# Row numbers of a paged gather moved one stage forward, and the sample rows' gate product moved ahead of a transpose

## The chip, the cores and the metric

The kernel is one program on one core of a Trainium2 chip. The metric is device time in microseconds (us), the median of the runs. Lower is better.

## The reference, cut to what matters

One layer of a hybrid decoder works on 2048 prompt rows and on 32 sample rows (8 entries of 4 new tokens, each with a past of 8192 tokens held in 64 pages of 128 tokens).

```python
k_past = cache_k_sb[i][page_table].reshape(dec_b, past, N_HEADS_SB, HEAD_DIM)
v_past = cache_v_sb[i][page_table].reshape(dec_b, past, N_HEADS_SB, HEAD_DIM)
...
o_sb = _stick_breaking(qa, k_all, v_all, pos_s, kpos_s, sb_bias[i])
...
def _merge(x, o_sb, z_sb, o_dl, z_dl, p, ...):
    y_sb = _rmsnorm(o_sb, out_norm_sb) * silu(z_sb)      # 512 columns
    y_dl = _rmsnorm(o_dl, out_norm_dil) * silu(z_dl)     # 512 columns
    x = x + einsum('bse,ed->bsd', concatenate([y_sb, y_dl]), w_out)
    gate = sigmoid(einsum('bsd,de->bse', x, w_ple_gate))
    return x + gate * einsum('bsp,pd->bsd', p, w_ple)
```

The paged keys and values of the sample rows are found through `page_table`. Every row, prompt or sample, then goes through the merge.

## The kernel before

The program runs seven stages one after the other: two projections, stick-breaking attention of the prompt (`sbp`), dilated attention of the prompt (`dil`), stick-breaking attention of the sample rows over the paged cache (`sbs`), dilated attention of the sample rows (`dls`), and the merge. A stage is a block in which each engine has its own ordered list of instructions, tied to the others by semaphores. All engines meet at a barrier between two stages, so nothing of a stage runs before the last engine has left the one ahead. Only the buffer `held` and a few semaphores live across stages.

**Dilated prompt stage (`dil`).** It goes over 80 work items g: four head pairs of 20 items each. In step g of its list, TensorE turns the weights of item g (L1363), scores item g + 2 (L1381, L1390), weighs item g - 1 (L1409) and turns out the sum of item g - 2 (L1418). VectorE in the same step copies turned weights (L1223), takes the maxima of item g + 2 (L1233), scales and writes out item g - 2 (`put_out`, L1267) and copies the sum of item g - 1 (`take_out`, L1254, L1258). TensorE waits for that last copy (`oT_copied`) before it opens the next sum in the bank `O`. GpSimd reorders the turned queries and keys for the next head pair (L1183, four casts of 128x2048) and issues the output transfers of each branch. SyncE (SP) issues the loads. At its start SP issues ident, masks, the values of two branches and the odd queries and keys, and then waits.

**Paged sample stage (`sbs`).** GpSimd gathers pages with indirect transfers of 128 rows of 8 KB each (L1560), into rings of eight slots for keys and eight for values. The row numbers come from the tile `rows`: SP loads the page table spread over 128 partitions (L1545) and a lane number for each partition (L1547); VectorE casts the table to floating point in four pieces of 32 partitions (L1582) and makes `page * 32 + lane` (L1585); GpSimd waits for that before its first gather. VectorE only then goes on with its own list: two memsets (L1587, L1588), the padded queries (L1600), and a short chain with ScalarE and TensorE over the new tokens (L1604 to L1624). TensorE multiplies padded queries and new keys (L1776) and, when that chain is through, starts to turn the gathered keys (L1793). Then come 32 steps of turning, scoring (L1837), a cumulative sum, exponentials and weighing (L1825).

**Merge.** Tile 0 holds the 32 sample rows, tiles 1 to 16 hold 128 prompt rows each. `prepare(i)` on VectorE and ScalarE makes y(i) out of loaded inputs (from L2332 to L2367). TensorE turns y(i) (L2556, `turn_y`), multiplies with w_out in two halves (`project_out`, `merge_Out`), turns x1(i) and p(i) (`turn_x1`, `turn_p`), and multiplies with w_ple_gate and w_ple (`gate_ple`, 48 matmuls into `merge_Gate` and 12 into `merge_Ple`). Every product is split in three (L2548 to L2550). All three kinds of transposes share one pair of banks, `merge_T`, which ScalarE (L2481) and VectorE (L2375, `low`) copy out. The order on TensorE in step i is:

```python
turn_x1(i - 1); project_out(i, 0); turn_p(i - 1); project_out(i, 1)
turn_y(i + 1)
gate_ple(i - 1)
```

`turn_x1(i)` waits for the residual sums of tile i (L2390). `turn_p(i)` waits for `low` of x1(i), which frees the first bank. VectorE's order in step i is `final_min(i - 2)` (L2396), `final_max(i - 2)` (L2401), `low` of x1(i - 1), `final_sum(i - 2)`, `low_p(i - 1)`, `low` of y(i + 1), `residual(i)`, `prepare(i + 2)`. In step 1 `prepare(2)` stands before `low` of y(2). ScalarE's list has the matching order, with the exponential of the gate product (`gate_in`) behind `prepare`.

Of the kernel before, what the change touches and what calls it, by code (L numbers as in the profile page):

```python
# [6 lines left out]
F32 = mybir.dt.float32  # L7
# [968 lines left out]


def paged_constants(held):
# [25 lines left out]

def dilated_prompt(nc, t, held, dil_qk_loaded, paged_loaded):

# [59 lines left out]
    with ctx:  # L1066
# [16 lines left out]
        lse = m.sb("lse", [P, 2, TILES, 2])  # L1083
        o_out = m.sb("o_out", [P, 2, TILES, P])
        Z = m.ps("Z", [P, 4, 512])
        ps_T = m.ps("ps_T", [P, 2, 512])
# [4 lines left out]
        masks_loaded = m.sem("masks_loaded")  # L1091
        consts_r = m.sem("consts_r")
        v_loaded = m.sems("v_loaded", 2)
        qk_odd_loaded = m.sem("qk_odd_loaded")
# [30 lines left out]
        def _(sp):  # L1125
# [11 lines left out]
            load_v(1)  # L1137
            load_dilated_qk(sp, t, qk_odd, 1, qk_odd_loaded)
            sp.wait_ge(turned, FILLS)
            load_dilated_qk(sp, t, held, 2, dil_qk_loaded)  # L1140
# [66 lines left out]
        def _(dve):  # L1207
# [52 lines left out]
            def put_out(g):  # L1260
# [4 lines left out]
                if x4 == 0 and b >= 2:  # L1265
# [4 lines left out]
                                        .to_broadcast([P, 8, DH]), ALU.mult).then_inc(o_scaled, 1)  # L1270

            for f in range(FILLS):
                low(0, f, Z[:, f % 4, :])
            for g in range(-2, G + 2):
                if 0 <= g < G and not short(g):
                    copy_weights(g)
# [174 lines left out]

def stick_breaking_sample(nc, t, held, paged_loaded):

# [15 lines left out]
    with ctx:  # L1469
# [3 lines left out]
            views[n] for n in ("ident", "own", "pick", "newer", "every", "spread", "bias", "fresh", "qk_new", "v_new"))  # L1473
        every_table = m.sb("every_table", [P, DEC_B * PAGES], I32)
        page_f = m.sb("page_f", [P, DEC_B * GROUPS])
        rows = m.sb("rows", [P, DEC_B * GROUPS], I32)
        lane = m.sb("lane", [P, 1])
        ones = m.sb("ones", [P, CK])
# [25 lines left out]

        lanes_loaded = m.sem("lanes_loaded")
        rows_step = m.sem("rows_step")
        zeroed = m.sem("zeroed")
# [35 lines left out]
        @block.sync  # L1543
        def _(sp):
            sp.dma_start(every_table[:, :], t["page_table"].rearrange("b n -> (b n)").rearrange("(a n) -> a n", a=1)  # L1545
                         .to_broadcast([P, DEC_B * PAGES])).then_inc(lanes_loaded, 16)
            sp.dma_start(lane[:, :], t["lane"][:, :]).then_inc(lanes_loaded, 16)  # L1547
            for b in range(DEC_B):
                sp.wait_ge(row_copied, b + 1)
                sp.dma_start(t["o_sb_s"][b * DEC_S:(b + 1) * DEC_S, :], o_row[:, :]).then_inc(stored, 16)  # L1550
            sp.wait_ge(stored, 16 * DEC_B)

        @block.gpsimd
        def _(pool):
            pool.wait_ge(rows_step, 2)

# [21 lines left out]
        def _(dve):  # L1578
            dve.wait_ge(lanes_loaded, 32)
            for i in range(GP):  # L1580
                r = slice(LANES * i, LANES * (i + 1))
                pages = nc.vector.tensor_copy(page_f[r, :], every_table[r, :].rearrange("p (n g) -> p g n", g=GP)[:, i, :])  # L1582
            pages.then_inc(rows_step, 1)
            dve.wait_ge(rows_step, 1)
            nc.vector.tensor_scalar(rows[:, :], page_f[:, :], float(LANES), lane[:, 0:1], ALU.mult, ALU.add) \  # L1585
                .then_inc(rows_step, 1)
            nc.vector.memset(q_pad[:, :, :], 0.0).then_inc(zeroed, 1)  # L1587
# [550 lines left out]
def merge(nc, t):  # L2138
# [6 lines left out]
    with ctx:  # L2145
# [396 lines left out]
        def _(pe):  # L2542
# [74 lines left out]
            for i in range(N + 1):  # L2617
# [6 lines left out]
                if i < N:  # L2624
                    project_out(i, 1)
                if i + 1 < N:
                    turn_y(i + 1)
                if i >= 1:
                    gate_ple(i - 1)


def build(nc, t):
# [8 lines left out]
    with nc.semaphore("tick") as tick:  # L2641
# [4 lines left out]
        paged_loaded = nc.alloc_semaphore(name="paged_loaded")  # L2646
        with nc.sbuf_tensor("held", [P, 2 * TILES * P], F32) as held:
# [3 lines left out]
            dilated_prompt(nc, t, held, dil_qk_loaded, paged_loaded)  # L2651
            stick_breaking_sample(nc, t, held, paged_loaded)
        nc.clear_and_free_semaphores([dil_qk_loaded, paged_loaded] + ahead_loaded + pair_loaded)
        nc.all_engine_barrier()
# [78 lines left out]
```

## Time and profile before

| what | value |
|---|---|
| median of 3 runs | 3076.78 us (3069.73 to 3077.31) |
| the profiled execution's own time | 3099.58 us |
| its span | 3097.9 us |
| TensorE busy in the span | 2808.1 us (91%) |
| VectorE, ScalarE, GpSimd busy | 1572.5, 1344.4, 749.7 us |
| mean granted TensorE clock | 0.959 of full speed |

The span is the part of the profiled execution between its first and its last instruction; 1.7 us lie around it. The profiled execution is 22.8 us longer than the median of the runs that were not profiled. Busy shares are means over seven stages with different limits.

### The profile page before, as it was taken

To read this page: it belongs to the slowest core of one execution; us is meant where nothing else is said; L and a number is where in the kernel's file an instruction comes from. 1 tells how busy PE (TensorE), PEld (TensorE's weight loads), DVE (VectorE), ACT (ScalarE), POOL (GpSimd) and SP (SyncE) were. 2 spreads that over 40 slices of the span, in tenths; PEclk is the share of its full clock that TensorE was granted. 3 is DMA by queue.
4 is the path that set the end of the run, shared out by engine and by line. 5 is a ranking of instruction groups with operands and counts; after the bars stand their busy time and mean duration, and the time that the engine had idled before them with its cause. 6 is when DMAs were issued, how large, how long until landed. Compare 5 with 4: busy or idle time off the path is not lost. (4 is left out here: it accounts for less than half of the span.)

```text
span 3097.9 us, 47359 instructions
## 1 busy us (share of the span) xinstructions
PE 2808.1 (91%) x17542; PEld 1978.9 (64%) x17542; DVE 1572.5 (51%) x2730; ACT 1344.4 (43%) x2482; POOL 749.7 (24%) x952
## 2 busy tenths in 40 slices
PE   7999989999899999998999758888888774899998
PEld 5888858888655555554888645555555442688887
DVE  3000032222588888887777633444434335666663
ACT  3212131111487777786677523333333323333332
POOL 0000001111122222223577733333333100000000
PEclk9999999999899999999999969999999987899999
DMA  6565766556300000103333389999999695323321
GB/s 209 200 215 197 235 209 210 183 203 217 112 15 28 15 28 1 42 8 100 97 84 84 80 339 407 416 419 417 408 414 407 252 374 217 126 100 108 108 87 43
DMA packets 209768, 574.16 MB, mean 185 GB/s; under 512 B 40096, under 2 KB 109184, under 8 KB 173728
## 3 DMA queue, kind: packets, MB, share of 16 engines
q0 software_dynamic: 45568, 348.22, 28.9%
q1 hardware_dynamic: 164000, 223.27, 21.9%
q8 instruction: 126, 2.06, 0.3%
q14 instruction: 74, 0.61, 0.1%
HBM read 494.67 MB, written 143.73 MB: 206 GB/s over the span
## 5 line engine op out<-in xcount | busy, mean ns | idle before, releaser
L495 PE MATMUL proj_ps_G<-proj_w_hi,proj_xT_hi 128*128 128x512 f32 x1024 | 399.8, 390 | 1.6 <-DVE proj_xT_lo L352 1.6
L499 PE MATMUL proj_ps_G<-proj_w_hi,proj_xT_lo 128*128 128x512 f32 x1024 | 398.6, 389 | 0.0
L497 PE MATMUL proj_ps_G<-proj_w_lo,proj_xT_hi 128*128 128x512 f32 x1024 | 398.5, 389 | 0.0
L1632 DVE COPY sbs_kT<-sbs_ps_T 128x512 f32<-128x512 f32 x256 | 173.7, 687 | 360.1 <-PE sbs_ps_T L1793 351.1
L434 ACT ACTIVATE proj_out<-proj_ps_G,proj_stat 128x512 f32<-128x512 f32 (+1 forms) x136 | 93.4, 688 | 579.5 <-PE proj_ps_G L499 574.8
L1793 PE MATMUL sbs_ps_T<-held,sbs_k_ring 128*128 128x128 f32 x2048 | 284.0, 297 | 26.8 <-ACT sbs_kT L1714 17.8
L1793 PEld LDWEIGHTS sbs_ps_T<-held,sbs_k_ring 128*128 128x128 f32 x2048 | 254.0, 155 | 64.2 <-issue 33.5
L695 POOL CAST sbp_sp_hi<-sbp_sp 128x512 fp32r<-128x512 f32 (+3 forms) x320 | 171.9, 551 | 455.8 <-DVE sbp_sp L742 455.6
L742 DVE SCALAR_TENSOR_TENSOR sbp_sp<-sbp_Z,sbp_el 128x512 f32<-128x512 f32 (+3 forms) x320 | 180.7, 606 | 88.9 <-ACT sbp_el L824 88.5
L495 PEld LDWEIGHTS proj_ps_G<-proj_w_hi,proj_xT_hi 128*128 128x128 f32 x1024 | 192.3, 188 | 41.4 <-DVE proj_xT_lo L352 1.8
L499 PEld LDWEIGHTS proj_ps_G<-proj_w_hi,proj_xT_lo 128*128 128x128 f32 x1024 | 192.2, 188 | 39.9
L497 PEld LDWEIGHTS proj_ps_G<-proj_w_lo,proj_xT_hi 128*128 128x128 f32 x1024 | 192.3, 188 | 39.3
L1714 ACT ACTIVATE sbs_kT<-sbs_ps_T 128x512 f32<-128x512 f32 x256 | 145.3, 591 | 152.8 <-PE sbs_ps_T L1793 151.7
L819 ACT ACTIVATE sbp_el<-sbp_Z 128x1024 f32<-128x1024 f32 (+3 forms) x160 | 143.6, 898 | 122.4 <-PE sbp_Z L908 121.2
L748 DVE TENSOR_TENSOR sbp_sp_lo<-sbp_sp,sbp_sp_hi 128x512 fp32r<-128x512 f32 (+3 forms) x320 | 192.0, 639 | 0.0
L352 DVE TENSOR_TENSOR proj_xT_lo<-proj_ps_T,proj_xT_hi 128x512 fp32r<-128x512 f32 (+1 forms) x34 | 21.1, 663 | 318.0 <-ACT proj_xT_hi L421 318.0
L1560 POOL DMA_INDIRECT sbs_v_ring<-in_cache_v_sb,sbs_rows x128 | 120.1, 939 | 256.5 <-PE sbs_O L1825 226.5
L1560 POOL DMA_INDIRECT sbs_k_ring<-in_cache_k_sb,sbs_rows x128 | 121.3, 948 | 168.9 <-PE sbs_ps_T L1793 139.2
L824 ACT ACTIVATE sbp_el<-sbp_el 128x1024 f32<-128x1024 f32 (+3 forms) x160 | 148.0, 925 | 0.0
L946 PE MATMUL sbp_L<-sbp_a,sbp_v_all 128*64 128x512 f32 (+3 forms) x640 | 145.8, 533 | 2.4 <-DVE sbp_LE L761 0.9
L831 ACT ACTIVATE sbp_a<-sbp_Z 128x1024 f32<-128x1024 f32 (+3 forms) x160 | 143.4, 896 | 9.9 <-PE sbp_Z L923 3.5
L1321 ACT ACTIVATE dil_sc<-dil_Z,dil_keep 128x256 f32<-128x256 f32 (+1 forms) x320 | 140.3, 462 | 3.2 <-DVE dil_keep L1233 3.2
(305 smaller groups left out, 5694.0 us busy)
## 6 DMA issues: line engine op xcount, KB each, us to landing
out_k_win_s<-in_cache_k_win POOLq DMA_DIRECT2D x16, 2044.0 KB
out_v_win_s<-in_cache_v_win POOLq DMA_DIRECT2D x16, 2044.0 KB
dls_k_in<-in_cache_k_win SPq DMA_DIRECT2D x16, 1024.0 KB, 10.7
dls_v_in<-in_cache_v_win SPq DMA_DIRECT2D x16, 1024.0 KB, 14.6
proj_out<-in_w_in SPq DMA_DIRECT2D x28, 512.0 KB, 5.0
merge_o<-scratch_o_dil SPq DMA_DIRECT2D x48, 256.0 KB, 4.8
proj_x_in<-in_x_prompt SPq DMA_DIRECT2D x16, 512.0 KB, 4.4
scratch_xT_hi<-proj_xT_hi SPq DMA_DIRECT2D x16, 512.0 KB, 4.8
```

The lines of the kernel that those rows point to most:

```text
L495: nc.tensor.matmul(ps_G[0:n, g, :], xT_hi[:, slot, k, 0:n], w_hi[:, k, cols], start=(k == 0), stop=False)
L497: nc.tensor.matmul(ps_G[0:n, g, :], xT_hi[:, slot, k, 0:n], w_lo[:, k, cols], start=False, stop=False)
L499: mm = nc.tensor.matmul(ps_G[0:n, g, :], xT_lo[:, slot, k, 0:n], w_hi[:, k, cols], start=False, stop=(k == KC - 1))
L695: nc.gpsimd.tensor_copy(sp_hi[:, b, h, c:512], sp_[:, g % 3, h, c:512]).then_inc(hi_done, 1)
L742: nc.vector.scalar_tensor_tensor(out=sp_[:, g % 3, h, c:512], in0=Z[:, z(g), h, c:512], scalar=LINEAR, in1=el[:, b, h, c:512], op0=ALU.max ...
L748: nc.vector.tensor_tensor(sp_lo[:, b, h, c:512], sp_[:, g % 3, h, c:512], sp_hi[:, b, h, c:512].bitcast(F32), ALU.subtract).then_inc(lo_do ...
L824: nc.scalar.activation(el[:, g % 2, :, c:512], el[:, g % 2, :, c:512], ACT.Ln, bias=1.0).then_inc(ln_done, 1)
L946: mm = nc.tensor.matmul(L[h * DH:(h + 1) * DH, c:512], v_all[:, j, p * P + h * DH:p * P + (h + 1) * DH], a[:, g % 2, h, c:512], start=True ...
L1560: pool.indirect_dma_start(ring[:, q % RING, :, :].rearrange("p g c -> p (g c)"), None, pages[0].rearrange("n (s g) h d -> (n s) (g h d)", ...
L1632: nc.vector.tensor_copy(kT[:, j, i, :], ps_T[:, x % TB, :]).then_inc(kT_odd, 1)
L1714: nc.scalar.activation(kT[:, j, i, :], ps_T[:, x % TB, :], ACT.Copy).then_inc(kT_even, 1)
L1793: tr = nc.tensor.transpose(by_lane[:, g_in, :], k_ring[:, q % RING, g_in, i * P:(i + 1) * P], ident[:, :])
```

## The change

Two edits. The first moves the making of the row numbers: `rows` becomes a buffer that lives across stages, the two loads are issued by SP in the dilated stage behind its first loads, and VectorE makes the numbers there at the top of step g = 20. The paged stage starts without them. The second edit puts `gate_ple(0)` ahead of `turn_y(2)` in step 1 of the merge. All other steps keep their order.

```diff
 def dilated_prompt(nc, t, held, rows, dil_qk_loaded, paged_loaded, rows_ready):
...
             load_dilated_qk(sp, t, qk_odd, 1, qk_odd_loaded)
+            sp.dma_start(every_table[:, :], t["page_table"].rearrange("b n -> (b n)").rearrange("(a n) -> a n", a=1)
+                         .to_broadcast([P, DEC_B * PAGES])).then_inc(lanes_loaded, 16)
+            sp.dma_start(lane[:, :], t["lane"][:, :]).then_inc(lanes_loaded, 16)
             sp.wait_ge(turned, FILLS)
...
+            def page_rows():
+                dve.wait_ge(lanes_loaded, 32)
+                for i in range(PAGES_A_GATHER):
+                    r = slice(PAGE // PAGES_A_GATHER * i, PAGE // PAGES_A_GATHER * (i + 1))
+                    pages = nc.vector.tensor_copy(page_f[r, :], every_table[r, :].rearrange("p (n g) -> p g n", g=PAGES_A_GATHER)[:, i, :])
+                pages.then_inc(pages_done, 1)
+                dve.wait_ge(pages_done, 1)
+                nc.vector.tensor_scalar(rows[:, :], page_f[:, :], float(PAGE // PAGES_A_GATHER), lane[:, 0:1], ALU.mult, ALU.add) \
+                    .then_inc(rows_ready, 1)
...
             for g in range(-2, G + 2):
+                if g == 20:
+                    page_rows()
                 if 0 <= g < G and not short(g):
                     copy_weights(g)
...
 def stick_breaking_sample(nc, t, held, rows, paged_loaded, rows_ready):
...
         def _(sp):
-            sp.dma_start(every_table[:, :], t["page_table"].rearrange("b n -> (b n)").rearrange("(a n) -> a n", a=1)
-                         .to_broadcast([P, DEC_B * PAGES])).then_inc(lanes_loaded, 16)
-            sp.dma_start(lane[:, :], t["lane"][:, :]).then_inc(lanes_loaded, 16)
...
         def _(pool):
-            pool.wait_ge(rows_step, 2)
+            pool.wait_ge(rows_ready, 1)
...
         def _(dve):
-            dve.wait_ge(lanes_loaded, 32)
-            for i in range(GP):
-                r = slice(LANES * i, LANES * (i + 1))
-                pages = nc.vector.tensor_copy(page_f[r, :], every_table[r, :].rearrange("p (n g) -> p g n", g=GP)[:, i, :])
-            pages.then_inc(rows_step, 1)
-            dve.wait_ge(rows_step, 1)
-            nc.vector.tensor_scalar(rows[:, :], page_f[:, :], float(LANES), lane[:, 0:1], ALU.mult, ALU.add) \
-                .then_inc(rows_step, 1)
             nc.vector.memset(q_pad[:, :, :], 0.0).then_inc(zeroed, 1)
...
                 if i < N:
                     project_out(i, 1)
+                if i == 1:
+                    gate_ple(0)
                 if i + 1 < N:
                     turn_y(i + 1)
-                if i >= 1:
+                if i > 1:
                     gate_ple(i - 1)
```

## Rows read from the trace of the kernel before

**Rows 1.** The page, part 1: busy time, share of the span and instructions.

```profile
PE 2808.1 (91%) x17542; PEld 1978.9 (64%) x17542; DVE 1572.5 (51%) x2730; ACT 1344.4 (43%) x2482; POOL 749.7 (24%) x952
```

**Rows 2.** Waits of the paged stage, 1900 to 2400 us: total, times, longest.

```profile
POOL sbs_k_ring L1560 <- PE sbs_ps_T L1793: 98.8, 59, 4.1
...
PE sbs_ps_T L1793 <- ACT sbs_kT L1714: 12.5, 24, 0.5
```

**Rows 3.** Windows of the paged stage: busy time, instructions, clock, DMA share, GB/s.

```profile
1808.00:1813.00 5.00, 0.00 (x0) 0.00 (x0) 1.93 (x7) 0.83 (x2) 0.00 (x0) 0.50 1.02 428
...
2000.00:2100.00 100.00, 84.47 (x684) 52.12 (x682) 42.42 (x70) 33.86 (x62) 37.15 (x40) 0.98 1.01 419
```

**Rows 4.** Timeline where the paged stage begins: start, duration, engine, line; idle time and releaser.

```profile
1787.93 1.28 ACT L62 ACT_TABLE_LOAD   x1 [24.89 <-PEq L45]
...
1791.35 1.09 DVE L1582 CAST sbs_page_f<-sbs_every_table 32x128 f32<-32x128 int32 x4 [21.47 <-DMA sbs_lane<-in_lane]
1792.48 0.29 DVE L1585 TENSOR_SCALAR sbs_rows<-sbs_page_f,sbs_lane 128x128 int32<-128x128 f32 x1
1792.98 1.12 DVE L1587 MEMSET sbs_q_pad<- 128x1280 f32 x1 [0.21 <-issue]
1793.05 1.06 POOL L1560 DMA_INDIRECT sbs_k_ring<-in_cache_k_sb,sbs_rows  x1 [10.84 <-DVE sbs_rows L1585]
```

**Rows 5.** Timeline, the end of the paged stage's opening chain.

```profile
1809.97 0.47 DVE L1604 TENSOR_SCALAR sbs_zn<-sbs_ps_T,held 32x256 f32<-32x256 f32 x1 [11.57 <-DMA proj_rope<-in_rope]
...
1817.01 1.33 PE L1793 MATMUL sbs_ps_T<-held,sbs_k_ring 128*128 128x128 f32 x5 [0.64 <-DVE sbs_aT_new L1624]
```

**Rows 6.** Timeline where the next stage (`dls`) begins.

```profile
2477.95 1.28 ACT L62 ACT_TABLE_LOAD   x1 [2.99 <-PEq L2654]
2478.28 1.12 DVE L1991 MEMSET dls_q_pad<- 128x1280 f32 x1 [5.02 <-PEq L2654]
```

**Rows 7.** Dilated stage: one window, then the timeline around step g = 20.

```profile
1529.00:1604.00 75.00, 75.00 (x832) 62.53 (x831) 58.58 (x103) 51.84 (x188) 55.03 (x51) 1.00 0.37 100
...
1532.85 7.82 POOL L1183 CAST dil_D_hi<-dil_T_hi 128x2048 fp32r<-128x2048 f32 x2
1534.62 0.64 DVE L1223 COPY dil_pT<-dil_ps_T 128x512 f32<-128x512 f32 x1
...
1537.77 0.68 DVE L1254 COPY dil_oT<-dil_O 128x512 f32<-128x512 f32 x1
...
1539.31 0.88 PE L1409 MATMUL dil_O<-dil_pT,dil_v_br 128*64 128x128 f32 x12
...
1540.61 7.86 POOL L1183 CAST dil_D_lo<-dil_T_lo 128x2048 fp32r<-128x2048 f32 x2
```

**Rows 8.** Timeline, a VectorE instruction of 256 elements in the paged stage.

```profile
1814.15 0.28 DVE L1619 TENSOR_SCALAR sbs_an<-sbs_an 32x256 f32<-32x256 f32 x1
```

**Rows 9.** Timeline of TensorE in the merge, steps 1 and 2.

```profile
2647.97 0.39 PE L2550 MATMUL merge_Out<-merge_wo_hi,merge_yT_lo 128*128 128x512 f32 x1
2659.16 1.97 PE L2556 MATMUL merge_T<-merge_ident,merge_y 128*128 128x128 f32 x8 [10.80 <-DVE merge_y L2367]
...
2675.55 1.03 PE L2556 MATMUL merge_T<-merge_ident,merge_x 128*128 128x128 f32 x8
...
2681.89 0.38 PE L2556 MATMUL merge_T<-merge_ident,merge_p_in 128*128 128x128 f32 x2
...
2687.59 1.03 PE L2556 MATMUL merge_T<-merge_ident,merge_y 128*128 128x128 f32 x8
2688.38 0.47 PE L2548 MATMUL merge_Gate<-merge_wg_hi,merge_xT_hi 128*128 128x512 f32 x1
...
2702.11 1.03 PE L2556 MATMUL merge_T<-merge_ident,merge_x 128*128 128x128 f32 x8
```

**Rows 10.** Timeline of VectorE in the merge, step 2.

```profile
2691.26 0.16 DVE L2332 TENSOR_TENSOR merge_top<-merge_lse 128x8 f32<-128x8 f32 x1
...
2704.30 1.28 DVE L2375 TENSOR_TENSOR merge_xT_lo<-merge_T,merge_xT_hi 128x512 fp32r<-128x512 f32 x2
```

More of the change, by code:

```diff
@@ L975, in load_dilated_qk @@
         sp.dma_start(view[:, i, :, :], src.rearrange("(n p) c -> p n c", p=P)[:, :, p * P:(p + 1) * P]).then_inc(loaded, 16)
+PAGES_A_GATHER = 4
+GROUPS_OF_PAGES = PAGES // PAGES_A_GATHER
 def paged_constants(held):
@@ L1002, in load_paged_constants, with dilated_prompt @@
             .then_inc(loaded, 16)
-def dilated_prompt(nc, t, held, dil_qk_loaded, paged_loaded):
+def dilated_prompt(nc, t, held, rows, dil_qk_loaded, paged_loaded, rows_ready):
     DILS = (1, 4, 16)
@@ L1084, in dilated_prompt @@
         o_out = m.sb("o_out", [P, 2, TILES, P])
+        every_table = m.sb("every_table", [P, DEC_B * PAGES], I32)
+        page_f = m.sb("page_f", [P, DEC_B * GROUPS_OF_PAGES])
+        lane = m.sb("lane", [P, 1])
         Z = m.ps("Z", [P, 4, 512])
@@ L1092, in dilated_prompt @@
         consts_r = m.sem("consts_r")
+        lanes_loaded = m.sem("lanes_loaded")
+        pages_done = m.sem("pages_done")
         v_loaded = m.sems("v_loaded", 2)
@@ L1449, in _, with stick_breaking_sample @@
                         turn_in(p + 1, f, OB[:, :])
-def stick_breaking_sample(nc, t, held, paged_loaded):
+def stick_breaking_sample(nc, t, held, rows, paged_loaded, rows_ready):
     C = H * DEC_S
@@ L1473, in stick_breaking_sample @@
             views[n] for n in ("ident", "own", "pick", "newer", "every", "spread", "bias", "fresh", "qk_new", "v_new"))
[L1474 to L1477, printed above, removed]
         ones = m.sb("ones", [P, CK])
@@ L1503, in stick_breaking_sample @@
         R = m.ps("R", [P, 512])
-        lanes_loaded = m.sem("lanes_loaded")
-        rows_step = m.sem("rows_step")
         zeroed = m.sem("zeroed")
@@ L2646, in build @@
         paged_loaded = nc.alloc_semaphore(name="paged_loaded")
-        with nc.sbuf_tensor("held", [P, 2 * TILES * P], F32) as held:
+        rows_ready = nc.alloc_semaphore(name="rows_ready")
+        with nc.sbuf_tensor("held", [P, 2 * TILES * P], F32) as held, \
+                nc.sbuf_tensor("rows", [P, DEC_B * GROUPS_OF_PAGES], I32) as rows:
             project(nc, t, 0, held, ahead_loaded, pair_loaded)
@@ L2650, in build @@
             stick_breaking_prompt(nc, t, held, pair_loaded, dil_qk_loaded)
-            dilated_prompt(nc, t, held, dil_qk_loaded, paged_loaded)
-            stick_breaking_sample(nc, t, held, paged_loaded)
-        nc.clear_and_free_semaphores([dil_qk_loaded, paged_loaded] + ahead_loaded + pair_loaded)
+            dilated_prompt(nc, t, held, rows, dil_qk_loaded, paged_loaded, rows_ready)
+            stick_breaking_sample(nc, t, held, rows, paged_loaded, rows_ready)
+        nc.clear_and_free_semaphores([dil_qk_loaded, paged_loaded, rows_ready] + ahead_loaded + pair_loaded)
         nc.all_engine_barrier()
```

## The prediction

> **What bounds the kernel now.** I read the page first. TensorE is busy for 91% of the span and VectorE for 51% [rows 1], but that is a mean over seven stages, and both edits touch places where TensorE stands still. So I went on by stage.
>
> In the paged stage the DMA engines are full (share 1.01, 419 GB/s) and TensorE is busy for 84 of 100 us [rows 3]. The waits tell which of the two paces it: GpSimd's gathers wait for TensorE's turned keys (98.8 us in 500), while TensorE's own waits are ended by ScalarE, VectorE or nothing that shows, none of them by a gather [rows 2]. The full DMA share follows the steps, it does not set them. Either way the stage has a fixed length from its opening on, so time saved in the opening comes off the end.
>
> The opening: the barrier lets the engines go at 1787.93, where ScalarE loads its table. VectorE has nothing to do until the lane numbers land at 1791.35, makes the row numbers until 1792.77, and only at 1792.98 begins the memset that heads its own chain. GpSimd's first gather goes at 1793.05 [rows 4]. The chain ends with the first turned key at 1817.01, which waited for VectorE (`sbs_aT_new`) and not for the gather issued 24 us earlier [rows 4, 5].
>
> In the dilated stage TensorE is busy for 75.00 of 75 us around step g = 20 and VectorE for 58.58 [rows 7]. TensorE is the bound; VectorE has some 16 us of slack in 75.
>
> In the merge TensorE stands still for 10.80 us ahead of `turn_y(2)`, waiting for y(2) [rows 9].
>
> **Edit 1, the row numbers.** *What goes from the paged stage*: two loads and five VectorE instructions. The next stage shows what an opening without them looks like: ScalarE's table load at 2477.95 and the same memset of 128x1280 at 2478.28, 0.33 us later [rows 6]. So the memset moves from 1792.98 to 1787.93 + 0.33 = 1788.26: 4.72 us earlier. The first gather moves by about as much, so the gathers, the memsets and the padded queries keep their places relative to each other. What would be late next is the first key: it has the same 24 us as before. Bounds: at most 1792.98 - 1787.93 = 5.05 us, at least nothing, if something else holds the chain. I take 4.7.
>
> The chain holds one stretch I cannot explain: VectorE waits 11.57 us until 1809.97 for the small product of L1776, while the DMA engines are full at 428 GB/s [rows 3, 5]. I leave it as long as it is; a rival takes it up.
>
> *What comes to the dilated stage*: SP issues two more loads behind its first ones, ahead of a wait that it reaches in either case; the numbers are wanted only in the second quarter of the stage's 80 items. VectorE gets the same five instructions: 1792.77 - 1791.35 = 1.42 us [rows 4]. They stand ahead of the copy at 1534.62, so that `take_out(19)`, seen at 1537.77, is pushed back. VectorE loses part of the 1.42 us again in its own short waits (0.29 and 0.32 us between these two), so about 0.65 us is left: the copy ends at 1537.77 + 0.68 + 0.65 = 1539.10. TensorE wants it at 1539.31 [rows 7]. Cost 0 by 0.2 us; if no wait were given back it would be 1.42 - (1539.31 - 1538.45) = 0.56 us. Cover gone altogether: 1.42 us. I take 0. GpSimd waits on a semaphore that has long been set.
>
> One cover could be false. From 1532.85 to 1548.47 GpSimd runs its four casts of some 3.9 us [rows 7], next to the moved VectorE instructions; in the old place it stood idle. The Trainium skill ("SBUF — State Buffer", section "SBUF: two separate sides") says that VectorE and GpSimd share a port pair under an exclusive lock, which a VectorE copy, cast or tensor_scalar takes in its two-port mode, and that the loser blocks for the whole instruction. By that rule the sum would lose up to what rival A gives, if these five ran in that mode. The rows speak against it: the five take 0.26 to 0.29 us for 128 elements a lane [rows 4], and a tensor_scalar with twice as many takes 0.28 [rows 8], so the moved ones run at half the rate of that one, one element at a time. A duration from the old place should hold.
>
> **Edit 2, the gate product ahead of `turn_y(2)`.** *What fills the idle time*: TensorE is through with `project_out(1, 1)` at 2648.2 [rows 9]. `gate_ple(0)` has what it needs by then (x1, p and all weights are split) and takes 2702.11 - 2688.38 = 13.73 us at full clock: 48 + 12 matmuls at 0.229 us [rows 9]. It ends at 2661.9. y(2) was ready at about 2659.1, so `turn_y(2)` starts at 2661.9, 2.8 us later than before.
>
> *What is late next.* In the old order `gate_ple(0)` lay over the work that ScalarE and VectorE do behind `turn_y(2)`. Now nothing does. VectorE's list is strict: low of y(2), residual(1), prepare(3), final_min(0), final_max(0), low of x1(1). In a warm step prepare begins 2691.26 - 2687.59 = 3.67 us after the turn starts, and low of x1 begins 2704.30 - 2691.26 = 13.04 us after that [rows 9, 10]. From 2661.9:
> - `turn_x1(1)` waits for residual(1): 2661.9 + 3.7 = 2665.6, so TensorE idles 2.9 us behind the turn. It then turns and does half a projection, 2681.89 - 2675.55 = 6.3 us [rows 9], until 2671.9.
> - `turn_p(1)` waits for low of x1(1), first half: 2661.93 + 3.67 + 13.04 + 0.69 = 2679.3. TensorE idles 7.4 us more.
>
> Before, `turn_p(1)` stood at 2681.89. So the idle 10.80 us come back as 2.9 + 7.4 = 10.3 us, and the gain up to here is 2681.9 - 2679.4 = 2.5 us, most of it the slow start of the old order: from 2659.16 the same work took 2675.55 - 2659.16 = 16.39 us against 2702.11 - 2687.59 = 14.52 us [rows 9], 1.87 us lost at half clock (1.2 instead of 2.4 GHz) after the idle stretch. A new idle stretch of 7 us should cost the same again. Net 2.5 - 1.9 = 0.6 us. Bounds: a gain of 2.5 us if the clock holds, a loss of 2 x 1.87 - 2.5 = 1.2 us if the slow stretch costs twice what it cost before. From `turn_y(3)` on the order and the slack are those of before.
>
> **Sum.** 4.7 - 0.0 + 0.6 = 5.3 us. The profiled execution, 3099.58 us, would be 3094.3. It lies 22.8 us above the median of the unprofiled runs; I take the difference over as it is: 3076.8 - 5.3 = 3071.5 us. A measurement of this kernel tells about 0.3%, or 9.2 us, from no change.
>
> **The rivals.**
>
> *A, the port (ends slower).* The five VectorE instructions are held until GpSimd's four casts are through: from 1534.6 to 1548.5, 13.9 us, less the 1539.31 - 1538.45 = 0.9 us that TensorE has. TensorE loses 13.0 us in a stage that it bounds; with the gain of 5.3 the time is 3076.8 + 13.0 - 5.3 = 3084.5. It decides the sign from a hold of 6.2 us on; a hold by one cast (3.9 us) leaves a gain of 2. For it: the casts do lie there. Against it: the durations above. By the Trainium skill's rule on the exclusive port pair the same 3084.5 follows if the mode is the two-port one.
>
> *B, the opening does not move.* Something else, such as the start of the first gathers beside the memset, holds the chain, and 1817.01 stays. Then only the merge's 0.6 us is left: 3076.2. Against it: the next stage opens without delay [rows 6].
>
> *C, the unexplained wait goes too.* If the wait until 1809.97 was a matter of how the chain meets the full DMA engines, it may shrink with another placing. Worth up to some 8 of its 11.57 us: 3076.8 - 5.3 - 8 = 3063.5. Against it: gathers and chain move together.
>
> *D, the merge's idle stretch is gained in full.* If VectorE and ScalarE kept up, TensorE would be late by the 2.9 us only: 10.8 + 1.9 - 2.9 = 9.8 us instead of 0.6, and 3062.3 in all. Against it: VectorE's 13.04 us, which no edit shortens.
>
> **How the numbers follow.** My forecast 0.70 (its own range 3067 to 3075.5, for a median of a few runs that spread over 7.6 us), A 0.05, B 0.11, C 0.08, D 0.04, other things 0.02. The range from 3063.5 to 3078.5 takes in the forecast and B and the near part of C, and leaves out D, A and the far part of C: under 2 in 10. Faster by over 0.3%: C and D, 0.12, and 0.03 for a forecast that measures long, 0.15. Slower by over 0.3%: A gives 0.25%, so only its upper part and chance, 0.04. Within: 0.81.
>
> **What would show it.** In the profile after: no VectorE instruction of L1582 or L1585's kind in the paged stage, its memset 0.3 us behind the table load and the first gather next to it; the distance from memset to first turned key 24.0 us as before. In the dilated stage the five instructions at 0.26 to 0.29 us, and TensorE without a gap behind them (a gap of some us and instructions of 3.9 us would be A). In the merge `merge_Gate` directly behind `merge_Out`, then a gap of about 2.9 us ahead of the turning of x1(1) and one of about 7 us ahead of that of p(1), with the granted clock at 0.5 behind it. I am wrong if that second gap is missing, or if the opening's chain is longer than before.

## The result, and the profile after

The changed kernel takes 3083.64 us (median of 7 runs, 3080.36 to 3091.52), the kernel before 3075.51 us (7 runs beside it, 3069.73 to 3077.31). The ratio is 1.0034, with a 95% interval of 1.0024 to 1.0043: slower by 0.34%, some 10.4 us (the two medians lie 8.1 us apart). I had forecast 3071.5 us and a range from 3063.5 to 3078.5. The measured time lies outside it, and rival A, to which I gave 0.05, is what happened.

The profiled execution of after took 3091.52 us with a span of 3089.9 us. That is less than the 3099.58 us of the one trace of before, though the kernel is slower. So totals of these two traces can't be set against each other, and I went by stages. A stage begins where ScalarE loads its table, as in [rows 4] and [rows 6]:

| stage, us | before | after |
|---|---|---|
| dilated prompt (1440.17 to 1787.93; 1444.12 to 1807.90) | 347.8 | 363.8 |
| paged stage | 690.0 | 660.6 |
| of it the opening, table load to first turned key | 29.1 | 16.4 |
| dilated sample | 106.3 | 108.2 |
| merge | 513.6 | 513.2 |

The dilated stage is 16.0 us longer. The 29.5 us that the paged stage lost look like a large gain. The experiments show that the change made 4 to 5 of them, and that the rest is a difference between sets of runs, which the kernel before shows too. A set is a group of kernels run one after the other on one chip. The first set ran on one chip, the second and third both on another, and two probes, of one execution each, on one more.

The page of after, engine totals, against [rows 1]. VectorE is busy for 12.6 us more with the same 2730 instructions, and that is the only hint in it of what happened:

```profile
PE 2800.7 (91%) x17542; PEld 1967.0 (64%) x17542; DVE 1585.1 (51%) x2730; ACT 1345.5 (44%) x2482; POOL 751.2 (24%) x952
```

**The dilated stage.** VectorE's timeline of after around step g = 20 (start, length, engine, line, operation, what it writes and reads, count), against [rows 7]:

```profile
1538.48 0.68 DVE L1266 COPY dil_oT<-dil_O 128x512 f32<-128x512 f32 x1
1539.19 14.50 DVE L1288 CAST dil_page_f<-dil_every_table 32x128 f32<-32x128 int32 x4
1553.72 0.29 DVE L1291 TENSOR_SCALAR rows<-dil_page_f,dil_lane 128x128 int32<-128x128 f32 x1
1553.92 0.68 DVE L1235 COPY dil_pT<-dil_ps_T 128x512 f32<-128x512 f32 x1
```

The four table casts take 14.50 us in place of about 1.1 [rows 4]. The view of that one line (least, median and longest, in ns) shows that it is one instruction, the first; the other three have their usual length:

```profile
L1288 DVE CAST dil_page_f<-dil_every_table x4: 262/320/13554, 1539.2 to 1553.4; 32x128 f32<-32x128 int32 x4
```

GpSimd's timeline of after in the same stretch:

```profile
1537.43 7.70 POOL L1195 CAST dil_D_hi<-dil_T_hi 128x2048 fp32r<-128x2048 f32 x2
1545.07 7.54 POOL L1195 CAST dil_D_lo<-dil_T_lo 128x2048 fp32r<-128x2048 f32 x2
1552.51 3.74 POOL L1179 DMA_DIRECT2D scratch_o_dil<-dil_o_out  x7
```

Its casts run back to back from 1537.43 to 1552.6, and VectorE's first cast begins 1.8 us into them and ends when they do: 1539.19 + 13.55 = 1552.74. It waited through four GpSimd instructions, not one. What it cost TensorE, from the windows of after (length, then busy time and count of PE, PEld, DVE, ACT, POOL, then granted clock, DMA share, GB/s):

```profile
1529.00:1539.00 10.00, 10.00 (x108) 8.23 (x104) 9.03 (x17) 6.86 (x25) 7.55 (x9) 1.00 1.16 311
1539.00:1554.00 15.00, 3.13 (x37) 2.48 (x36) 14.92 (x8) 2.33 (x9) 15.00 (x7) 0.76 0.35 98
1556.00:1557.00 1.00, 1.00 (x6) 0.38 (x4) 1.00 (x3) 1.00 (x6) 1.00 (x3) 0.50 0.40 131
...
1554.00:1604.00 50.00, 49.25 (x498) 40.38 (x498) 37.14 (x65) 32.37 (x116) 34.16 (x38) 0.93 0.24 64
```

TensorE does 37 matmuls in the 15 us instead of some 160 (it does 108 in the 10 us ahead of them), and nothing makes up for it. Note that a busy VectorE (14.92 of 15) is here an engine that stands still. TensorE's timeline of after shows two parts of the price:

```profile
1541.53 0.60 PE L1387 MATMUL dil_ps_T<-dil_ident,dil_sc 128*128 128x128 f32 x4
1554.75 1.08 PE L1387 MATMUL dil_ps_T<-dil_ident,dil_sc 128*128 128x128 f32 x4 [12.62 <-DVE dil_pT L1235]
...
1558.19 1.55 PE L1433 MATMUL dil_O<-dil_pT,dil_v_br 128*64 128x128 f32 x12
...
1562.89 1.09 PE L1433 MATMUL dil_O<-dil_pT,dil_v_br 128*64 128x128 f32 x16
```

It stands still for 12.62 us, until VectorE's next copy, that of the turned weights (`dil_pT`). Then, until about 1561, it runs at the lower of its two clocks (granted 0.50, which is 1.2 GHz): 12 matmuls of L1433 take 1.55 us, 0.129 each, where 16 take 1.09, 0.068 each, at full clock. Half of the 6 us from 1554.75 on are lost as well, some 3 us by this estimate. From GpSimd's first cast to its end the stage takes 270.5 us, against 255.1 in before, so the hold cost 15.4 us, and 12.6 + 3 is that but for a few tenths. The other 0.6 us of the 16.0 lie ahead of the cast.

**The opening of the paged stage.** The timeline of after, with the idle time ahead of an instruction and what ended it in brackets; against [rows 4, 5]:

```profile
1807.90 1.28 ACT L62 ACT_TABLE_LOAD   x1 [24.92 <-PEq L45]
1808.24 1.12 DVE L1594 MEMSET sbs_q_pad<- 128x1280 f32 x1 [18.43 <-PEq L45]
1808.68 1.06 POOL L1575 DMA_INDIRECT sbs_k_ring<-in_cache_k_sb,rows  x1 [6.51 <-POOLq L45]
...
1813.73 3.34 PE L1783 MATMUL sbs_ps_T<-sbs_kT_new,sbs_q_pad 128*32 128x32 f32 x64 [4.76 <-DVE sbs_q_pad L1607]
1817.10 0.47 DVE L1611 TENSOR_SCALAR sbs_zn<-sbs_ps_T,held 32x256 f32<-32x256 f32 x1 [3.43 <-PE sbs_ps_T L1783]
...
1824.32 0.47 PE L1800 MATMUL sbs_ps_T<-held,sbs_k_ring 128*128 128x128 f32 x1 [0.64 <-DVE sbs_aT_new L1631]
```

The memset stands 0.34 us behind the table load (forecast 0.33), the first gather 0.44 us behind the memset. From memset to first turned key it takes 16.08 us; I had forecast 24.0. All of that is the wait for the small product, 3.43 us in place of 11.57 [rows 5].

The trace of before shows what the long wait is made of:

```profile
1798.45 3.06 PE L1776 MATMUL sbs_ps_T<-sbs_kT_new,sbs_q_pad 128*32 128x32 f32 x52 [9.46 <-DVE sbs_q_pad L1600]
...
1805.47 0.31 PE L1776 MATMUL sbs_ps_T<-sbs_kT_new,sbs_q_pad 128*32 128x32 f32 x2 [0.51 <-issue]
```

Here TensorE runs 52 of the product's 64 matmuls in one go and the last 12 in pieces until 1805.78, with pauses in which it waits for nothing that the profile shows ("issue"). VectorE then starts only 4.2 us later. In after all 64 run in one go, and VectorE starts right behind them.

**The merge.** TensorE's timeline of after, against [rows 9]:

```profile
2639.72 0.39 PE L2555 MATMUL merge_Gate<-merge_wg_hi,merge_xT_hi 128*32 128x512 f32 x1
...
2653.62 0.60 PE L2563 MATMUL merge_T<-merge_ident,merge_y 128*128 128x128 f32 x4
...
2657.42 1.09 PE L2563 MATMUL merge_T<-merge_ident,merge_x 128*128 128x128 f32 x8 [2.77 <-DVE merge_x L2397]
...
2671.11 0.66 PE L2563 MATMUL merge_T<-merge_ident,merge_p_in 128*128 128x128 f32 x2 [7.11 <-DVE merge_xT_lo L2382]
...
2679.45 1.04 PE L2563 MATMUL merge_T<-merge_ident,merge_y 128*128 128x128 f32 x8
```

The 10.80 us came back as 2.77 and 7.11 us, each ended by the buffer that I named (forecast 2.9 and 7.4). From the end of `project_out(1, 1)` to `turn_y(3)` it takes 2679.45 - 2639.72 = 39.73 us, before 2687.59 - 2648.20 = 39.39 us.

### The profile page after: what moved, and what is told of

Its sections match the earlier page's. It is cut to its first block and busy times, and to the rows that moved or that the text cites. A ratio compares the mean times of both kernels' runs of the same rounds, so it can differ in the third digit from the quotient of the medians.

```text
span 3089.9 us, 47359 instructions
## 1 busy us (share of the span) xinstructions
PE 2800.7 (91%) x17542; PEld 1967.0 (64%) x17542; DVE 1585.1 (51%) x2730; ACT 1345.5 (44%) x2482; POOL 751.2 (24%) x952
## 5 line engine op out<-in xcount | busy, mean ns | idle before, releaser
L1800 PE MATMUL sbs_ps_T<-held,sbs_k_ring 128*128 128x128 f32 x2048 | 260.6, 283 | 16.7 <-ACT sbs_kT L1721 16.1
L1800 PEld LDWEIGHTS sbs_ps_T<-held,sbs_k_ring 128*128 128x128 f32 x2048 | 235.5, 147 | 50.4 <-issue 26.2
L1575 POOL DMA_INDIRECT sbs_v_ring<-in_cache_v_sb,rows x128 | 120.4, 941 | 289.3 <-PE sbs_O L1832 259.3
L1575 POOL DMA_INDIRECT sbs_k_ring<-in_cache_k_sb,rows x128 | 122.0, 953 | 105.2 <-PE sbs_ps_T L1800 87.1
## 6 DMA issues: line engine op xcount, KB each, us to landing
dls_v_in<-in_cache_v_win SPq DMA_DIRECT2D x16, 1024.0 KB, 14.7
```

Source lines behind the costliest of these rows:

```text
L1575: pool.indirect_dma_start(ring[:, q % RING, :, :].rearrange("p g c -> p (g c)"), None, pages[0].rearrange("n (s g) h d -> (n s) (g h d)", ...
L1800: tr = nc.tensor.transpose(by_lane[:, g_in, :], k_ring[:, q % RING, g_in, i * P:(i + 1) * P], ident[:, :])
```

## The experiments

My theory for them was rival A as it came: the whole loss is one VectorE instruction held while GpSimd casts, worth about 15 us; the opening gives 4 to 5 back; the merge gives nothing. Rivals: that the longer list of VectorE or the two added loads cost something wherever they stand; that the merge's new order costs; that the large gain of the paged stage is the change's, and something unseen costs more.

### The kernel before, once more

> The kernel before, unchanged, for a second profile and a null measurement. Theory of the chance trace: the one trace of before was unusual in the paged stage (690 us long, against 661 us in the changed kernel); this one shows 665 to 675 us there, and the ratio is 1.000 within its interval. Rival, the opening: the placing of the gathers against the chain sets the length of the steps; then this paged stage is again some 690 us long.

Measured: 3093.56 us (12 runs), beside 3096.15 us of the same kernel as comparison (33 runs), ratio 0.9987, 0.9973 to 1.0001. So two measurements of one kernel in one set agree within 0.13%. Its dilated stage takes 347.4 us, as in the first trace: the 16.0 us are the change's. Its timeline, the same opening:

```profile
1788.58 1.28 ACT L62 ACT_TABLE_LOAD   x1 [24.88 <-PEq L45]
...
1810.64 0.47 DVE L1604 TENSOR_SCALAR sbs_zn<-sbs_ps_T,held 32x256 f32<-32x256 f32 x1 [11.61 <-DMA proj_rope<-in_rope]
...
1817.67 0.47 PE L1793 MATMUL sbs_ps_T<-held,sbs_k_ring 128*128 128x128 f32 x1 [0.64 <-DVE sbs_aT_new L1624]
```

It repeats the first trace to 0.1 us (opening 29.09), so my theory that this trace was a chance execution, with a paged stage of 665 to 675 us elsewhere, fell: the stage takes 683.6 us here. The same kernel has a median of 3096.15 us in this set of runs and of 3075.51 us in that of the result. The set matters, and every kernel is to be read beside others of its set.

### The rows alone, and the merge alone

Rows alone is the changed kernel with the merge's old order; merge alone is the kernel before with

```
                if i < N:
                    project_out(i, 1)
+               if i == 1:
+                   gate_ple(0)
                if i + 1 < N:
                    turn_y(i + 1)
-               if i >= 1:
+               if i > 1:
                    gate_ple(i - 1)
```

> The changed kernel with the merge in its old order: the row numbers alone. Theory of the port: the dilated stage is 16 us longer than in the second profile of before, the paged stage at least 5 us shorter, the time is that of the changed kernel within 3 us (about 1.003 of before). Rival, the merge is to blame for the loss: then this kernel is at 0.998 or below.

> The kernel before with the gate product of the sample rows ahead of turn_y(2): the merge edit alone. Theory: two new idle stretches of 2.8 and 7.1 us take the place of the one of 10.8 us, the time is that of before within 1 us (ratio 0.999 to 1.001). Rival, the merge costs or gives back something outside these stretches: a ratio away from 1 by 0.002 or more.

Measured: rows alone 3105.44 us, 1.0035 (1.0023 to 1.0047), all of the loss; merge alone 3092.25 us, 0.9994 (0.9979 to 1.0008), nothing that can be told. The timeline of the rows alone:

```profile
1437.43 1.28 ACT L62 ACT_TABLE_LOAD   x1 [3.26 <-PEq L45]
...
1532.21 14.36 DVE L1288 CAST dil_page_f<-dil_every_table 32x128 f32<-32x128 int32 x4
...
1800.08 1.28 ACT L62 ACT_TABLE_LOAD   x1 [24.90 <-PEq L45]
...
1818.10 0.47 DVE L1611 TENSOR_SCALAR sbs_zn<-sbs_ps_T,held 32x256 f32<-32x256 f32 x1 [12.25 <-DMA sbp_v_all<-out_v_sb_p]
...
1825.13 0.47 PE L1800 MATMUL sbs_ps_T<-held,sbs_k_ring 128*128 128x128 f32 x1 [0.64 <-DVE sbs_aT_new L1631]
```

The dilated stage takes 362.6 us, 15.2 more than in the kernel before, run on the same chip. The opening takes 25.05 us, 4.0 less. And here, with the rows moved, VectorE waits 12.25 us for the small product: the long wait is not what the change removed.

### The five instructions at other places

First at step 16, where GpSimd has no casts; then behind the last step of the stage (both with the merge's old order):

```
-                if g == 20:
+                if g == 16:
                     page_rows()
```
```
-                if g == 20:
-                    page_rows()
...
                 if 0 <= g - 1 < G and CLOSES[(g - 1) % NI]:
                     take_out(g - 1)
+            page_rows()
```

> The row numbers alone, made at step g = 16 of the dilated stage instead of g = 20, where GpSimd waits for the next output and runs no cast. Theory of the port: the four casts of the table take 0.26 us each, the dilated stage is at most 1.5 us longer than before, the opening of the paged stage keeps its gain: 0.996 to 0.9985 of before. Rival, the five instructions cost the dilated stage 16 us wherever they stand (a late load of the table, say): 1.003 again.

> The row numbers alone, made at the end of VectorE's list in the dilated stage, where VectorE has nothing left to do for some 18 us and GpSimd only issues output transfers. Theory of the port: only GpSimd's own computing holds the five instructions, a held one would lie under GpSimd's tail anyway; the dilated stage is as long as before within 0.5 us, the opening of the paged stage 4 us shorter, the time 0.9985 to 0.999 of before. Rival, GpSimd's issuing of transfers holds VectorE too or is held by it: the five instructions are longer than 0.3 us or the stage ends later.

Measured: step 16 3089.64 us, 0.9988 (0.9976 to 1.0000), a little less than expected; at the end 3070.25 us, 0.9982 (0.9973 to 0.9991), before 3074.76 (26 runs). The timeline with step 16, VectorE and below it GpSimd:

```profile
1519.03 1.08 DVE L1288 CAST dil_page_f<-dil_every_table 32x128 f32<-32x128 int32 x4
1520.15 0.28 DVE L1291 TENSOR_SCALAR rows<-dil_page_f,dil_lane 128x128 int32<-128x128 f32 x1
...
1516.85 0.25 POOL L1166 TENSOR_TENSOR dil_lse<-dil_lse,dil_keep 128x32 f32<-128x32 f32 x1 [19.11 <-ACT dil_lse L1357]
...
1528.07 2.27 POOL L1179 DMA_DIRECT2D scratch_o_dil<-dil_o_out  x3 [10.97 <-DVE dil_o_out L1279]
```

Beside an idle GpSimd the casts have the length that they had in the old place [rows 4]. The stage takes 349.6 us, 2.2 more than in the kernel before on the same chip, and more than the 1.5 us that I allowed. That is not the five instructions: at 1516.85, before they start, the stage is 77.4 us old, where in the kernel before it is 75.2 us old at the same GpSimd instruction. The windows of the stage's first 20 us, first in the kernel before, then with step 16, show where it comes from:

```profile
1441.15:1461.15 20.00, 14.47 (x94) 11.71 (x94) 11.01 (x18) 11.16 (x28) 7.93 (x3) 0.74 1.04 272
1439.48:1459.48 20.00, 14.57 (x78) 11.49 (x80) 9.42 (x15) 9.38 (x22) 8.05 (x3) 0.62 1.01 264
```

The granted clock is 0.62 there in place of 0.74, and TensorE gets through 78 matmuls in place of 94. GpSimd's first cast of this head pair splits the stage cleanly (us):

| kernel | stage's start to the cast | the cast to the stage's end |
|---|---|---|
| before / before once more | 92.7 / 92.4 | 255.1 / 255.1 |
| rows at step 16 / at the end | 94.6 / 92.4 | 255.1 / 255.1 |
| rows on ScalarE / the same, with half the gate (both below) | 92.5 / 95.0 | 255.3 / 255.3 |
| after / rows alone at step 20 | 93.3 / 93.0 | 270.5 / 269.6 |
| two inputs / reduction (both below) | 92.7 / 92.8 | 269.5 / 255.1 |

The first part varies by 2.6 us between executions. The second is 255.1 to 255.3 us without a held instruction and 14.4 to 15.4 us longer with one. With the rows at the stage's end the stage takes 347.5 us, and the opening 16.54 us:

```profile
1785.61 1.28 ACT L62 ACT_TABLE_LOAD   x1 [24.90 <-PEq L45]
...
1795.11 0.47 DVE L1610 TENSOR_SCALAR sbs_zn<-sbs_ps_T,held 32x256 f32<-32x256 f32 x1 [3.72 <-PE sbs_ps_T L1782]
```

So the same five instructions and two loads cost 15 us at step 20, nothing that shows at step 16, none at the end: the place, not the work. The rival of a cost wherever they stand is out.

### The rows on ScalarE, at the same step

VectorE's five instructions leave the kernel; ScalarE makes the numbers at g = 20 (merge in the old order):

```
+                for i in range(PAGES_A_GATHER):
+                    r = slice(PAGE // PAGES_A_GATHER * i, PAGE // PAGES_A_GATHER * (i + 1))
+                    made = nc.scalar.activation(rows[r, :], every_table[r, :].rearrange("p (n g) -> p g n", g=PAGES_A_GATHER)[:, i, :],
+                                                ACT.Identity, scale=float(PAGE // PAGES_A_GATHER), bias=lane[r, 0:1])
+                made.then_inc(rows_ready, 1)
```

> The row numbers at step g = 20 again, beside GpSimd's casts, but made by ScalarE: four activations of 32 partitions that read the table, multiply by 32 and add the lane, in place of VectorE's five instructions. Theory of the port, which VectorE shares with GpSimd and ScalarE does not: no instruction is held, the dilated stage is at most 1.5 us longer than before, the time 0.998 to 0.9995 of before. Rival, the place and the data are to blame (a late table, a full queue): 15 us are lost again and the ratio is 1.003.

Measured: 3069.47 us, 0.9977 (0.9968 to 0.9987); dilated stage 347.7 us. The timeline, ScalarE and GpSimd:

```profile
1534.15 2.12 ACT L1353 ACTIVATE rows<-dil_every_table,dil_lane 32x128 int32<-32x128 int32 x4
...
1534.23 7.86 POOL L1195 CAST dil_D_hi<-dil_T_hi 128x2048 fp32r<-128x2048 f32 x2
```

Same step, same data, same GpSimd casts 0.08 us behind the start, and no hold: it belongs to VectorE.

### Which VectorE instructions are held, and at what rate they run

Three probes in the kernel before, each of which adds instructions whose results nothing uses. At the end of the dilated stage, to read the rate of longer versions (`by_three` takes every third element of a tile read as int32):

```
+            nc.vector.tensor_copy(probe[:, 0, :], by_three[:, 0, :])
+            nc.vector.tensor_copy(probe[:, 1, :], masks[:, 0, :].bitcast(I32))
+            nc.vector.tensor_copy(probe[:, 2, :], masks[:, 0, :])
+            nc.vector.tensor_scalar(probe_i[:, :], masks[:, 1, :], 32.0, ident[:, 0:1], ALU.mult, ALU.add)
+            nc.vector.tensor_copy(probe[:, 3, 0:128], by_three[:, 0, 0:128])
```

At step 20, beside the casts, one instruction with two inputs from SBUF, and in another kernel one with a single input that reduces:

```
+                if g == 20:
+                    nc.vector.tensor_tensor(probe[:, :], ident[:, :], masks[:, 0, 0:P], ALU.add)
```
```
+                if g == 20:
+                    nc.vector.tensor_reduce(probe[:, 0:1], masks[:, 0, 0:P], AX.X, ALU.add)
```

> The kernel before with five extra VectorE instructions that touch nothing else, at the end of VectorE's list in the dilated stage, where no GpSimd cast runs: an int32 to f32 cast of 128x512 with a stride of three elements, the same with unit stride, an f32 copy of 128x512, a tensor_scalar of 128x512 from f32 to int32 with a lane's operand, and the strided cast with 128 elements. They show at which rate each works. If the casts work at one element a cycle, as I read it off their 0.26 us, the 512-element ones take about 0.68 us; if at two, 0.42 us, and the evidence of the prediction was a misreading of a fixed cost.

> The kernel before with one extra VectorE instruction at the top of step g = 20: a tensor_tensor of 128x128 with both inputs in SBUF, beside GpSimd's casts. Theory by which any VectorE instruction that needs a second read of SBUF is held: it takes 13 us or so and the dilated stage is that much longer. Rival, only the casts and copies in the two-port mode are held: it takes 0.2 to 0.4 us and the stage keeps its length within 1 us.

> The kernel before with one extra VectorE instruction at the top of step g = 20: a tensor_reduce of 128x128 that reads one tile in SBUF and writes one number a lane, beside GpSimd's casts. Theory by which only an instruction that takes the second read or write of SBUF is held: it takes 0.2 to 0.3 us and the dilated stage keeps its length of 347.4 to 348.6 us. Rival, every VectorE instruction whose input lies in SBUF is held: 13 us again, and a stage of 362 us.

One execution each: rates 3079.23 us and two inputs 3092.19 us beside 3080.66 us of before; the reduction 3077.07 us beside 3080.4 (11 runs). The rates, from the timeline:

```profile
1774.59 0.49 DVE L1291 CAST dil_probe<-dil_masks 128x512 f32<-128x512 int32 x1
1774.99 0.50 DVE L1292 CAST dil_probe<-dil_masks 128x512 f32<-128x512 int32 x1
1775.41 0.41 DVE L1293 COPY dil_probe<-dil_masks 128x512 f32<-128x512 f32 x1
1775.74 0.47 DVE L1294 TENSOR_SCALAR dil_probe_i<-dil_masks,dil_ident 128x512 int32<-128x512 f32 x1
1776.14 0.23 DVE L1295 CAST dil_probe<-dil_masks 128x128 f32<-128x128 int32 x1
```

The strided cast takes 0.49 us for 512 elements and 0.23 us for 128: 0.26 us for 384 more. By these two points alone that is 0.68 ns each and 0.14 us that don't depend on the size. Of the two lengths that the expectation gives for 512 elements, 0.68 us (as the copies from PSUM take) and 0.42 us, it is nearer the short one, and at 128 elements more than half of its length says nothing of the rate. The two inputs beside GpSimd's casts, from the timeline:

```profile
1539.10 13.56 DVE L1277 TENSOR_TENSOR dil_probe<-dil_ident,dil_masks 128x128 f32<-128x128 f32 x1
...
1537.33 7.70 POOL L1184 CAST dil_D_hi<-dil_T_hi 128x2048 fp32r<-128x2048 f32 x2
```

The hold is the same to 0.01 us, for an instruction that casts nothing. The stage takes 362.2 us: this one probe in the kernel before gives nearly the whole loss of the changed kernel (14.4 us behind GpSimd's first cast, where after has 15.4). The reduction:

```profile
1531.77 0.24 DVE L1277 TENSOR_REDUCE dil_probe<-dil_masks 128x1 f32<-128x128 f32 x1
...
1530.01 7.84 POOL L1184 CAST dil_D_hi<-dil_T_hi 128x2048 fp32r<-128x2048 f32 x2
```

Same place, same source, 0.24 us, stage 347.9 us. The Trainium skill ("SBUF — State Buffer", section "SBUF: two separate sides") names both kinds that take the shared port pair: a VectorE instruction in a two-port mode, and one with two SBUF inputs against a GpSimd instruction that reads SBUF. The rows of the table cast (held), the two inputs (held) and the reduction (not held) agree with it. The page has the holder keep the pair for one whole instruction. The traces show a longer wait: 13.56 us, through four instructions of some 3.8.

### What the merge has to give

In the kernel before, `gate_half(0)` (24 of the gate's 48 matmuls) ahead of `turn_y(2)`, the rest and the 12 of `ple` behind it. Then the same with the rows at the stage's end, and with the rows on ScalarE:

```
                     project_out(i, 1)
+                if i == 1:
+                    gate_half(0)
                 if i + 1 < N:
                     turn_y(i + 1)
-                if i >= 1:
+                if i == 1:
+                    gate_rest(0)
+                if i > 1:
                     gate_ple(i - 1)
```

> The kernel before with only half of the sample rows' gate product (24 matmuls into the first bank, about 5.7 us) ahead of turn_y(2) and the other half and the small product behind it. Theory: the half fits into the idle 10.8 us without making turn_y(2) late, the rest still covers the work of ScalarE and VectorE behind it; turn_p(1) then waits for low of x1(1) and stands about 4.3 us earlier than in the old order, less 0 to 2.5 us for the clock: 0.9985 to 0.9995 of before, and the merge 2 to 4 us shorter in the profile. Rival, VectorE's list takes all of it again: the merge is as long as before.

> The row numbers at the end of VectorE's list and the halved gate product together. Both theories: the gains add up, 6 to 8 us, 0.9975 to 0.998 of before. Rival, one of them is taken back by the other: no better than the better of the two alone.

> The row numbers made by ScalarE at step g = 20 and the halved gate product together. Theory: the two gains add up as they did with the numbers at the end of the stage: 0.9965 to 0.9975 of before. Rival, the four ScalarE activations of 0.5 us each delay something that the merge's gain hides: 0.998.

Measured: half the gate 3071.16 us, 0.9982 (0.9973 to 0.9991); with the rows at the end 3065.64 us, 0.9966 (0.9952 to 0.9979); with the rows on ScalarE 3068.94 us beside 3080.4 (11 runs), 0.9954 (0.9938 to 0.9971). Each of the five kernels that gain (these three, the rows at the end and the rows on ScalarE) came out a little below the ratios that I expected, though each interval reaches into them. TensorE's timeline with half the gate alone, and VectorE's of its opening:

```profile
2636.64 1.97 PE L2556 MATMUL merge_T<-merge_ident,merge_y 128*128 128x128 f32 x8 [6.46 <-DVE merge_y L2367]
...
2654.92 0.41 PE L2556 MATMUL merge_T<-merge_ident,merge_p_in 128*128 128x128 f32 x2 [0.46 <-DVE merge_xT_lo L2375]
...
1805.83 0.47 DVE L1604 TENSOR_SCALAR sbs_zn<-sbs_ps_T,held 32x256 f32<-32x256 f32 x1 [3.71 <-PE sbs_ps_T L1776]
```

Ahead of `turn_y(2)` 6.46 us of the 10.80 are left, the work behind the turn still covers VectorE's chain, and the second gap is 0.46 us. The merge takes 508.2 us instead of 512.9 to 513.6, about 5 us less, more than the 2 to 4 that I expected. The third row is from a kernel with the rows in their old place: it too waits only 3.71 us. In this set of runs a kernel with the rows unmoved has the short wait too, so it came with the set.

The dilated stage and the opening of all of them (us); the sets of runs stand apart:

| kernel | dilated stage | opening |
|---|---|---|
| first set: before / merge alone | 347.4 / 348.1 | 29.1 / 29.2 |
| rows at step 20 / step 16 | 362.6 / 349.6 | 25.1 / 25.1 |
| second: half the gate | 347.6 | 21.3 |
| rows at the end / on ScalarE / at the end, with half | 347.5 / 347.7 / 348.1 | 16.5 / 16.4 / 16.5 |
| between them: probe of rates / two inputs | 348.6 / 362.2 | 21.0 / 21.3 |
| third: reduction / rows on ScalarE, with half | 347.9 / 350.2 | 28.9 / 24.8 |

In each set moving the rows out takes 4.0 to 4.8 us off the opening, on top of whichever wait the set has. The second and third set ran on the same chip, one with the short wait and one with the long, so the chip does not decide it. In every trace with the long wait the product's matmuls run in pieces, as in before, and in every trace with the short wait in one go. Behind the first turned key the paged stage takes 654.0 to 659.1 us in the first set, 642.0 to 643.9 in the second and in the probes, and 641.5 to 641.8 in the third: this larger difference doesn't go with the wait.

The last kernel is 0.46% faster than before, more than its parts: 4.1 (opening) and 4.4 (merge, 508.8 against 513.2) less 2.3 (dilated stage) make 6 us of the measured 14, and the interval's least gain is 8.9 us. The 2.3 us are the slow start of that one trace (95.0 us to the first cast) and not the change's. I don't account for the rest. It and the one with the rows at the end were measured in different sets of runs, and their intervals overlap; both beat the kernel before and the changed one, and I don't rank them.

## Why the prediction was wrong

- **The cost of the five moved instructions (taken as 0.0 us, bounded at 1.42 us): this step failed.** It measured 14.4 to 15.4 us. "A duration from the old place should hold", because they run "one element at a time", was wrong twice. First, the duration was misread. I compared 0.26 to 0.29 us for 128 elements [rows 4] with 0.28 us for 256 [rows 8] and took the ratio for a rate; the probe shows some 0.14 us of such an instruction to be independent of size, and 512 elements to take 0.49 us, not the 0.68 of one element at a time. The rows could not tell the modes apart, and I used them to rule one out. Second, I held that only one mode would be exposed, where the two-input probe is held just the same.
- **The cover.** I did see the casts beside the new place, named the rule, and priced the hold at 13.9 us (13.55 measured). The price and the sum of rival A, 3084.5 us, were near (3083.64 measured). Its terms measured +14.4 to 15.4, -4.0 to -4.8 and +0.3, which gives 9.9 to 11.7 us where A had 7.7, so the agreement of the totals is in part luck. The chance of 0.05 was the mistake. With a stage bound by TensorE and a price of 13 us against a gain of 5, an argument by analogy between two short durations should not have bought 14 to 1 against.
- **The size of the loss.** Rival A put it at 13.0 us with 0.9 us of slack. TensorE's gap is 12.62 us, but it came about otherwise. VectorE's copy of the turned weights was late by the whole 14.7 us from 1539.19 to 1553.92, of which the hold is 13.55, and TensorE had some 2.1 us of slack ahead of it, not the 0.9 ahead of `take_out`. The two errors nearly cancel. The stage lost 14.4 to 15.4 us in the three kernels with a hold. The term left out is the slow clock behind the gap, some 3 us, which I had charged in the merge and not here.
- **The opening (-4.7).** Right: -4.8 in the second set (21.3 to 16.5), which has the short wait as the trace of after does, and -4.0 and -4.1 in the others. Rival B fell.
- **The unexplained wait (rival C).** It did shrink in the trace of after, by 8.1 us, as C had it, but not by the change: the kernel before shows 3.71 us in one set, and moved rows show 12.25 us in another.
- **The merge (-0.6).** +0.3, inside my bounds of -2.5 to +1.2. The two gaps came where and as long as forecast. The term mis-sized was the slow start: from `turn_p(1)` to `turn_y(3)` it takes 2679.45 - 2671.11 = 8.34 us, against 5.70 in before [rows 9], so 2.6 us are lost at the lower clock where I took 1.9; the other 0.2 us are that `turn_p(1)` came 2.3 us earlier and not 2.5. Rival D fell.
- **The base.** I carried the 22.8 us between the trace and the median over as a constant. The same kernel has medians of 3075 and 3096 us in different sets, and the trace of before has the long wait and the long paged stage of the slower set, so the 22.8 us were most likely a difference of sets.

Left open: why the small product runs in pieces in some sets of runs, with a wait of some 11.6 us, and in one go in others, with 3.4 to 3.7; and why the paged stage behind the first turned key is 10 to 18 us longer in the first set. That a pause between GpSimd's casts would end the hold earlier wasn't tried.

## What to carry to other kernels

Ahead of moving a VectorE instruction, list what GpSimd does at the new place: if it reads SBUF there for long, a VectorE cast or two-input instruction between SBUF tensors can stand until GpSimd's whole run of instructions is through, however short it is itself. Put such work where GpSimd is idle, or on ScalarE. And read no rate off a 128-element instruction: compare two sizes, or give the hold the chance that its price deserves. Set a stage's two parts, ahead of the change and behind it, beside the old ones before laying a difference of its length on the change. Where idle time waits for another engine's chain, fill only as much of it as leaves that chain covered: half the gate gained 5 us, the whole nothing.

## What the runs showed of the hardware

- A VectorE instruction of 0.26 us, started 1.8 us into four GpSimd casts in a row, ended with the last of them (13.55 us); a two-input instruction in its place took 13.56 us, and the first table cast with the rows alone, whose four took 14.36 us together, 13.53. None of them got in between two of GpSimd's casts. The copies from PSUM beside the same casts were not held: 0.64 us [rows 7]. Nor was a reduction with one SBUF input (0.24 us), nor ScalarE's four activations on the same data (2.12 us together).
- The strided int32 to f32 cast in SBUF costs 0.68 ns an element and 0.14 us besides, by the two sizes probed; without a stride 512 elements take as long (0.50 against 0.49 us). An f32 copy of 512 takes 0.41 us.
- One kernel, the same stages: 3075.5, 3080.4 and 3096.2 us as medians in different sets of runs, with one wait of 3.7 or 11.6 us in the paged stage.
- The dilated stage's start varies by 2.6 us with the clock granted in its first 20 us (0.74 to 0.78 and 92 to 94 matmuls in the shortest, 0.50 and 70 matmuls in the longest); from GpSimd's first cast on it takes 255.1 to 255.3 us in every kernel without a hold.
